# Sliding-window attention inside a two-block kernel: values as split fp32r products, probabilities scaled before the transposes

## The reference

```
scores = q . k / 8 + bias                      (bias: slope * distance, or -1e30 outside the window)
probs  = softmax([scores, sink])[..., :-1]     (the sink is in the denominator only)
out    = probs . v                             (4 query heads share one key/value head)
attn   = out * silu(gate)
y      = [pool_out, attn] @ w_out
```

## Time and profile before

| what | value |
|---|---|
| median of three runs | 1696.41 us |
| profiled execution, span from first to last instruction | 1693.7 us |
| profiled execution's own time beside its span | not on the page; the median lies 2.7 us above the span |
| TensorE busy | 1672.2 us, 99% |
| VectorE, ScalarE, GpSimd busy | 839.8, 560.5, 510.7 us |
| sliding-attention loop on TensorE | 186.5 to 321.3 us |

### The profile page before, as it was taken

The page is one execution under the profiler, slowest core; times in us unless marked ns, Lnnn a source line. Parts: engine busy times, 40 slices in busy tenths (PEclk is TensorE's granted clock), DMA queues, the critical chain, the costliest instruction groups (busy, mean ns, idle before and its releaser), DMA issues.

```text
span 1693.7 us, 22505 instructions
## 1 busy us (share of the span) xinstructions
PE 1672.2 (99%) x8729; PEld 1385.6 (82%) x8729; DVE 839.8 (50%) x1622; ACT 560.5 (33%) x1280; POOL 510.7 (30%) x402
## 2 busy tenths in 40 slices
PE   7999999999999999999999999999999999999998
PEld 6778788889888787888888887888887999988886
DVE  4330255344253624568076752838412888855714
ACT  5101456334333003440034300441113777741111
POOL 6225033023333333022220232015314745534310
PEclk9999999999999999999999999999999999999999
DMA  6113022233267232111320223126465525226322
GB/s 207 51 64 110 13 63 71 88 115 100 74 209 272 92 118 79 35 35 52 109 91 23 69 71 106 44 80 241 162 218 162 136 57 137 57 67 218 107 112 100
DMA packets 97130, 178.44 MB, mean 105 GB/s; under 512 B 13912, under 2 KB 33792, under 8 KB 96896
## 3 DMA queue, kind: packets, MB, share of 16 engines
q1 hardware_dynamic: 61120, 95.57, 19.3%
q10 hardware_dynamic: 35904, 81.44, 13.7%
HBM read 122.05 MB, written 54.92 MB: 104 GB/s over the span
## 4 chain that ended last, share of the span: by engine, by line
PE 98%; DVE 1%; ACT 1%; DMA 0%; POOL 0%; issue 0%; DVEq 0%; POOLq 0%
PE ps L1224 24%; PE ps L1138 16%; PE ps L840 14%; PE ps L1074 5%; PE ps L1387 5%; PE ps L1327 5%; PE ps L1271 4%; PE ps L976 4%; PE ps L1357 4%; PE ps L1340 3%; PE ps L894 3%; PE ps L1239 2%; PE ps L1252 2%; PE ps L1028 2%; PE ps L1001 1%; PE ps L873 1%
## 5 line engine op out<-in xcount | busy, mean ns | idle before, releaser
L720 POOL TENSOR_SCALAR w_hi<-w_stage 128x1024 fp32r<-128x1024 f32 (+3 forms) x140 | 127.8, 920 | 964.1 <-PE ps L1224 359.8
L727 POOL TENSOR_TENSOR w_lo<-w_stage,w_hi 128x1024 fp32r<-128x1024 f32 (+3 forms) x140 | 269.8, 1934 | 8.9
L1224 PE MATMUL ps<-h2T_hi,w_hi 128*128 128x512 f32 x384 | 156.6, 408 | 0.3 <-issue 0.3
L1138 PE MATMUL ps<-h2T_hi,w_hi 128*128 128x512 f32 x384 | 153.4, 399 | 0.3 <-issue 0.3
L1138 PE MATMUL ps<-h2T_lo,w_hi 128*128 128x512 f32 x384 | 152.1, 396 | 0.0
L1224 PE MATMUL ps<-h2T_hi,w_lo 128*128 128x512 f32 x384 | 152.1, 396 | 0.0
L1138 PE MATMUL ps<-h2T_hi,w_lo 128*128 128x512 f32 x384 | 151.5, 394 | 0.0
L1224 PE MATMUL ps<-h2T_lo,w_hi 128*128 128x512 f32 x384 | 151.1, 394 | 0.0
L2308 DVE SCALAR_TENSOR_TENSOR rope_swapped<-ps,sin_table_T 32x512 f32<-32x512 f32 x192 | 131.9, 687 | 3.9
L1764 ACT ACTIVATE probs_dil<-probs_dil,dil_stats_out 128x256 f32<-128x256 f32 (+2 forms) x192 | 87.5, 457 | 104.3 <-DVE dil_stats_out L2333 104.3
L2441 DVE TENSOR_REDUCE small<-ps 128x1 f32<-128x1024 f32 x64 | 77.7, 1214 | 54.9 <-PE ps L1327 54.9
(11 more groups left out here) (296 smaller groups left out, 3745.7 us busy)
## 6 DMA issues: line engine op xcount, KB each, us to landing
w_stage<-in_w_in SPq DMA_DIRECT2D x76, 512.0 KB, 3.8
w_stage<-in_w_out SPq DMA_DIRECT2D x16, 512.0 KB, 3.8
gate_scr<-gate_tiles ACTq DMA_DIRECT2D x16, 512.0 KB, 3.6
gates<-gate_scr ACTq DMA_DIRECT2D x32, 256.0 KB, 3.2
v_dil<-v_dil_scr SPq DMA_DIRECT2D x25, 256.0 KB, 3.4
v_dil_scr<-values_out SPq DMA_DIRECT2D x24, 256.0 KB, 2.0
dil_scr<-dil_out SPq DMA_DIRECT2D x96, 64.0 KB, 1.6
dil_nums<-dil_scr ACTq DMA_DIRECT2D x24, 256.0 KB, 4.2
```

The costliest lines, as they stand in the source:

```text
L720: last = nc.gpsimd.tensor_scalar(hi_, raw_, 1.0, 0.0, ALU.mult, ALU.add)
L727: last = nc.gpsimd.tensor_tensor(lo_, raw_, hi_.bitcast(F32), ALU.subtract)
L1138: m = pe.matmul(ps[:, gate_bank(u), :], a[:, s, k, P * m_:P * m_ + P], b[:, k, COLS * n:COLS * n + COLS], start=(k == 0 and j == 0), stop= ...
L1224: m = pe.matmul(bank, a, b, start=(k == 0 and i == 0), stop=(k == KT - 1 and i == 2))
```

## The change

In the sliding attention:

- V is held as a pair of fp32r tiles (`vS`), high from ScalarE, low from VectorE, side by side in one stationary tile of 128 columns per key/value head.
- VectorE forms and inverts the sums right after the exponentials (`inverse`), and GpSimd multiplies the rows of the probabilities by them (`swa_norm`), before TensorE transposes them. The four transposes of one key block go to one bank.
- ScalarE copies the transposed probabilities as fp32r (`swa_high`), and VectorE the remainder (`swa_low`), per key block.
- Values: V is stationary, and two heads' probabilities (256 columns) stream, high then low; the result has channels in partitions. It lies in two alternating banks (4 and 5), and its high and low sums in different partitions: ScalarE copies one part across partitions into `qT`, whose columns of that tile are no longer needed (`swa_merge`), VectorE adds the other (`swa_total`), GpSimd multiplies by the gate (`swa_gate`).
- No transposes back; no division after the values.
- GpSimd's new steps are placed in its queue: steps 0 to 6 ahead of panel `o0`, the rest behind single chunks of `o0` and `o1` (`SWA_STEPS`).
- The pooled half's buffer becomes single, and its pieces come at other iterations. The first tile's output products wait for two chunks of their weight panel a part, rather than for four.

```diff
-    POOL_AT = (2, 4, 6, 8, 12, 13, 14, 15)
+    POOL_AT = (2, 4, 6, 8, 12, 14, 16, 18)
+    SWA_STEPS = ((7,), (8,), (9,), (10, 11), (12,), (), (13,), (14, 15, 16, 17))
+    def swa_blocks(i):
+        return min(i, HH) + 2 * max(i - HH, 0)
...
+        def swa_norm(i):
+            t, hh = divmod(i, HH)
+            nk = P if t == 0 else 2 * P
+            pool.wait_ge(*after("swa_recip", i + 1))
+            for j in range(G):
+                h = G * hh + j
+                last = nc.gpsimd.tensor_scalar(pr[:, i % 2, j, 0:nk], pr[:, i % 2, j, 0:nk], st[:, t % 2, 1, h:h + 1], 0.0,
+                                               ALU.mult, ALU.add)
+            last.then_inc(sem("swa_normed"), 1)
+        def swa_gate(i):
+            t, hh = divmod(i, HH)
+            tk = slice(P * t, P * t + P)
+            pool.wait_ge(*after("swa_sum", i + 1))
+            pool.wait_ge(*after("fill_evac", 4 if t < 4 else 12))
+            nc.gpsimd.tensor_tensor(aT[:, hh::2, tk], aT[:, hh::2, tk], qT[:, hh::2, tk], ALU.mult).then_inc(sem("swa_aT"), 1)
+        def swa_step(i):
+            if i < TT * HH:
+                swa_norm(i)
+            if i >= 2:
+                swa_gate(i - 2)
...
+            if p == index["o0"]:
+                for i in range(7):
+                    swa_step(i)
...
+                    if p in (index["o0"], index["o1"]):
+                        for i in SWA_STEPS[4 * (p - index["o0"]) + ci]:
+                            swa_step(i)
...
         def swa_transposes(i):
-            pe.wait_ge(*after("swa_exp", G * (i + 1)))
-            if i >= 1:
-                pe.wait_ge(*after("swa_pT", i))
-            for j in range(G):
-                for kb in range(nb):
-                    c = 2 * j + kb
-                    m = pe.transpose(ps[:, 2 + c // 4, (c % 4) * P:(c % 4) * P + P],
-                                     pr[:, i % 2, j, P * kb:P * kb + P], ident[:])
-            m.then_inc(sem("swa_T"), 1)
+            pe.wait_ge(*after("swa_normed", i + 1))
+            for kb in range(nb):
+                if i >= 1:
+                    pe.wait_ge(*after("swa_lo", swa_blocks(i) - (nb - 1 - kb if i > HH else 0)))
+                for j in range(G):
+                    m = pe.transpose(ps[:, 2 + kb, P * j:P * j + P], pr[:, i % 2, j, P * kb:P * kb + P], ident[:])
+                m.then_inc(sem("swa_T"), 1)
         def swa_values(i):
-            pe.wait_ge(*after("swa_pT", i + 1))
-            if i >= 1:
-                pe.wait_ge(*after("swa_out", i))
-            for j in range(G):
-                h = swa_head(G * hh + j)
-                for kb in range(nb):
-                    kt = t - nb + 1 + kb
-                    m = pe.matmul(ps[:, 4, HD * j:HD * j + HD], pT[:, 2 * j + kb, :],
-                                  v1[:, kt, HD * (h // 4):HD * (h // 4) + HD], start=(kb == 0), stop=(kb == nb - 1))
+            pe.wait_ge(*after("swa_lo", swa_blocks(i + 1)))
+            if i == 0:
+                pe.wait_ge(*after("v1_lo", 2))
+            if i >= 2:
+                pe.wait_ge(*after("swa_sum", i - 1))
+            for kv in range(2):
+                ops = [(vS[:, t - nb + 1 + kb, kv].rearrange("p a d -> p (a d)"),
+                        p_[:, G * kb + 2 * kv:G * kb + 2 * kv + 2, :].rearrange("p j q -> p (j q)"))
+                       for kb in range(nb) for p_ in (pTh, pTl)]
+                for x_, (a, b) in enumerate(ops):
+                    m = pe.matmul(ps[:, 4 + i % 2, 2 * P * kv:2 * P * kv + 2 * P], a, b, start=(x_ == 0), stop=(x_ == len(ops) - 1))
             m.then_inc(sem("swa_valued"), 1)
-        def swa_back(t):
...
         def out_part(t, half, part):
+            if t == 0:
+                pe.wait_ge(*after("w_split", chunk_end[index[name]] - 2 * (1 - part)))
...
+        def swa_high(i):
+            for kb in range(swa_blocks(i + 1) - swa_blocks(i)):
+                act.wait_ge(*after("swa_T", swa_blocks(i) + kb + 1))
+                if i >= 1 and kb == 0:
+                    act.wait_ge(*after("swa_valued", i))
+                act.activation(pTh[:, G * kb:G * kb + G, :], ps[:, 2 + kb, :].rearrange("p (j c) -> p j c", c=P),
+                               ACT.Copy).then_inc(sem("swa_hi"), 1)
+        def swa_merge(i):
+            t, hh = divmod(i, HH)
+            act.wait_ge(*after("swa_valued", i + 1))
+            src = ps[:, 4 + i % 2, :].rearrange("p (a x q) -> p a x q", a=2, x=2)
+            tk = slice(P * t, P * t + P)
+            act.activation(qT[0:HD, hh::2, tk], src[HD:P, :, 0, :], ACT.Copy).then_inc(sem("swa_merge"), 1)
+            act.activation(qT[HD:P, hh::2, tk], src[0:HD, :, 1, :], ACT.Copy).then_inc(sem("swa_merge"), 1)
...
+        def inverse(i):
+            t, hh = divmod(i, HH)
+            hs = slice(G * hh, G * hh + G)
+            dve.wait_ge(*after("swa_sink", i + 1))
+            in_turn(nc.vector.tensor_tensor(st[:, t % 2, 1, hs], st[:, t % 2, 1, hs], st[:, t % 2, 2, hs], ALU.add))
+            nc.vector.reciprocal(st[:, t % 2, 1, hs], st[:, t % 2, 1, hs]).then_inc(sem("swa_recip"), 1)
+        def swa_low(i):
+            for kb in range(swa_blocks(i + 1) - swa_blocks(i)):
+                dve.wait_ge(*after("swa_hi", swa_blocks(i) + kb + 1))
+                js = slice(G * kb, G * kb + G)
+                nc.vector.tensor_tensor(pTl[:, js, :], ps[:, 2 + kb, :].rearrange("p (j c) -> p j c", c=P),
+                                        pTh[:, js, :].bitcast(F32), ALU.subtract).then_inc(sem("swa_lo"), 1)
+        def swa_total(i):
+            t, hh = divmod(i, HH)
+            tk = slice(P * t, P * t + P)
+            src = ps[:, 4 + i % 2, :].rearrange("p (a x q) -> p a x q", a=2, x=2)
+            dve.wait_ge(*after("swa_merge", 2 * i + 2))
+            for x_, rows in enumerate((slice(0, HD), slice(HD, P))):
+                dst = qT[rows, hh::2, tk]
+                last = nc.vector.tensor_tensor(dst, src[rows, :, x_, :], dst, ALU.add)
+            last.then_inc(sem("swa_sum"), 1)
...
-            if u >= 2:
-                act.wait_ge(*after("pool_lo", u - 1))
+            if u >= 1:
+                act.wait_ge(*after("pool_lo", u))
...
+            if 2 <= i < steps + 2:
+                swa_merge(i - 2)
             if 1 <= i <= steps:
-                swa_pT(i - 1)
+                swa_high(i - 1)
...
-        for i in range(steps + 3):
-            if i < steps:
-                softmax_in(i)
-            if 2 <= i < steps + 2:
-                normalise(i - 2)
+        for i in range(steps + 4):
+            if 1 <= i <= steps:
+                inverse(i - 1)
+            if i < steps:
+                softmax_in(i)
+            if 2 <= i < steps + 2:
+                swa_total(i - 2)
             if i - 1 in POOL_AT:
                 pool_lo(POOL_AT.index(i - 1))
             if i >= 6 and i % 2 == 0:
                 attn_lo((i - 6) // 2)
-            if i >= 4 and i % 2 == 0:
-                back((i - 4) // 2)
+            if 1 <= i <= steps:
+                swa_low(i - 1)
```

More of the change, by code:

```diff
@@ L270, in hybrid_blocks_kernel @@
     kT = sb("k1T", [P, S], F32, s2)
-    vT = sb("v1T", [P, S], F32, s2)
-    v1 = sb("v1", [P, TT, P], F32, s2)
+    vS = sb("v1_pair", [P, TT, 2, 2, HD], F32R, s2)
     swa_b = sb("swa_bias", [P, H1, 2 * P], F32, s2)
     pr = sb("probs", [P, 2, G, 2 * P], F32, s2)
-    pT = sb("probsT", [P, 2 * G, P], F32, s2)
-    ao = sb("attn_tok", [P, H1, HD], F32, s2)
+    pTh = sb("probsT_hi", [P, 2 * G, P], F32R, s2)
+    s2v = ExitStack()
+    vT = sb("v1T", [P, S], F32, s2v)
+    s2v.close()
+    pTl = sb("probsT_lo", [P, 2 * G, P], F32R, s2)
     st = sb("attn_stats", [P, 2, 4, H1], F32, s2)
-    pmR = sb("pool_outT_back", [P, 2, COLS], F32, s2)
+    pmR = sb("pool_outT_back", [P, COLS], F32, s2)
     s2.close()
@@ L984, in _ @@
         pe.wait_ge(*after("qkv_evac", 8))
-        pe.wait_ge(*after("v1_evac", 2))
         def keys_of(t):
@@ L1063, in out_part @@
                 elif t == 2:
-                    pe.wait_ge(*after("swa_pT", steps))
+                    pe.wait_ge(*after("swa_lo", swa_blocks(steps)))
                 elif t == 3:
-                    pe.wait_ge(*after("swa_out", steps))
-                    pe.wait_ge(*after("swa_aT", TT))
+                    pe.wait_ge(*after("swa_sum", steps))
                 elif half == 0:
@@ L1484, in _ @@
                 for half in range(2):
-                    act.activation(v1[:, 4 * half:4 * half + 4, :], ps[:, 4 + half, :], ACT.Copy).then_inc(sem("v1_evac"), 1)
+                    act.activation(vS[:, 4 * half:4 * half + 4, :, 0, :], ps[:, 4 + half, :].rearrange("p (t a d) -> p t a d", t=4, a=2),
+                                   ACT.Copy).then_inc(sem("v1_hi"), 1)
         def fill_evac(f):
@@ L1517, in pool_in @@
-            act.dma_start(pmR[:, u % 2, :], pool_d[P * k:P * k + P, COLS * n:COLS * n + COLS]).then_inc(sem(f"pool_back{u % 2}"), 16)
+            if u >= 1:
+                act.wait_ge(*after("pool_lo", u))
```

(27 more changed lines are left out.)

43 lines of the change are left out of this document (10 added, 33 removed).

## The result

The changed kernel took 1703.6 us (median of 5 runs, 1701.75 to 1705.6) against 1696.7 of the kernel before: ratio 1.0041, 95% interval 1.0029 to 1.0052. It is slower by 6.9 us, or 0.4%. Its profiled execution has a span of 1702.3 us, 8.6 more than before.

A forecast was written before the change was run, and what follows sets the result against it. TensorE, 98% of the chain, was taken to bound the kernel. Loop terms -0.4 + 3.4 - 4.0 + 5.6 - 2.0 = +2.6 us on 1696.4 gave 1699.0; range 1692 to 1706.

The forecast's parts named there:

- What TensorE saves: Sliding attention: cheaper values save 11.8 us, dropped transposes back 3.5, together 15.3 if nothing waits.
- Steps 8 to 11: Loop steps with two half projections: TensorE's own 8.7 us each covers the ring, so -4.0 us.
- Steps 0 to 2: Start of the sliding attention loop: cheaper first-tile values gain 0.4 us ahead of score step 3.
- Steps 16 to 18: End of the loop: two values and transposes back less, up to 0.7 us lost to last scalings, -2.0.
- Steps 3 to 7: Early loop steps: step 3 at 5.9 us, then four turns of 7.7 with hold-up; +3.4 us.
- the ring: Sliding attention loop: masking, exponentials, merges, totals, low halves, sum and reciprocal wait in a circle; 7.6 us, or 7.0.
- The second hold: Loop transposes wait for GpSimd's four scalings, 2.1 us after the low halves; step about 7.2 us even with a shorter ring.
- VectorE and GpSimd: In the loop these engines hold each other up: 0 to 0.7 us a turn, taken as 0.2; 1.8 late.
- Steps 12 to 15: Late loop steps: GpSimd's queue of scalings, gates and o1 chunks sets the length, 33.2 us against 27.6; +5.6.
- rival 2: Slower by GpSimd: scalings cost 0.56 us or merges 0.6; about +7, 1703.4 us; chance 0.34.
- Rival 1: Faster: engines hand over sooner, the ring closes in 6.6 us and chunks fit between; -8.6, 1687.8 us; chance 0.17.
- Rival 3: TensorE's clock falls in the loop's new gaps, its work taking 11.8 us a step; +33, 1729 us; chance 0.03.

The follow-up runs named there:

- e6: e8 with VectorE's low halves moved ahead of the masking and ScalarE's high copies ahead of the merges; 1684.2 us.
- e1: Changed kernel with VectorE reordered (masking, low halves of step i-2, totals of step i-3) and GpSimd's gate products one step later; 1692.5 us.
- e0: Changed kernel with VectorE's pooled or attention low half moved behind the low halves of the probabilities; 1700.9 us.
- e4: Changed kernel without GpSimd's scalings, so rows are not divided by their sums; 1701.4 us.
- e7: Changed kernel with the reorderings of e1 and e2 together and without GpSimd's scalings; 1690.1 us.
- e2: Changed kernel with only GpSimd's order changed: gate products one step later, panel o1's four chunks ahead of scalings 11 to 14; 1700.1 us.
- e8: Changed kernel with the reorderings of e1 and e2 together, plus VectorE's pooled or attention low half ahead of the totals; 1686.6 us.

## Why the prediction was right and wrong

The mechanism was as forecast in steps 3 to 7 and only in part in the late steps, and its size was short: 1699.0 against 1703.6, inside the range. "Within 0.2%" was the likeliest of the three outcomes, and the kernel came out 0.4% slower. By its steps:

- **What TensorE saves**: right. Eight values take 0.96 (322.47 in the chain) for the forecast 0.94. With most of its waits gone (e6), 12.7 of the 15.3 us come out as time.
- **Steps 8 to 11**: -4.0 forecast, -4.0 measured. **Steps 0 to 2**: -0.4 and -0.4. **Steps 16 to 18**: -2.0 and -1.6.
- **Steps 3 to 7**: +3.4 forecast, +5.2 measured: step 3 took 6.5 instead of 5.9, the four turns 32.0 instead of 30.8. This is the step that failed most by size: the ring was the right cause (e1, e0), but 7.6 should have been 8.19, and 7.0 without the low half 7.47. Masking with its add took 2.03 (forecast 1.90), the merges 0.79 (0.65), the totals 0.86 (0.70), the low half beside them 0.7 (0.6). I took a tenth off each pair for overlap; in this chain no pair overlapped (two merges of 0.38 and 0.39 took 0.79), and each handover added some 0.02 to 0.1. The exponentials' rows make 2.18, not the 2.15 of my sum; they took 2.17. The eight steps that can move had a mean of 8.23 instead of 8.0.
- **The second hold**: wrong as a bound. Its terms make 2.0 and 6.9, not 2.1 and 7.2, and the turn that it was to set is the ring's 7.47. Scalings at 0.46 instead of 0.40 make it no shorter, but e4 shows that without them the turn loses 0.1, and e7 that the open step loses nothing. The 9.2 us put down to them in the waits are the ring's.
- **VectorE and GpSimd**: 0.2 a turn forecast in steps 4 to 7, 0.1 measured (the add at 214.62, 0.28 instead of 0.16); in the late steps 1.8 in all forecast, 3.1 measured, and there it moves with the order of either engine (e2, e8).
- **Steps 12 to 15**: +5.6 forecast, +6.3 to 6.4 measured, for another reason, so that the near miss is in part luck. I took GpSimd for the only bound there, "busy without a pause". In the trace it pauses twice for 2.2 us, for VectorE's reciprocal, and TensorE waits for o1's split for only 0.8 in all: what paces these steps is the ring, with two hold-ups in it (e2), and GpSimd's queue is the next bound (e1). Within GpSimd's sum, what failed is "counted from scores 12": I let the chunk start 5.2 us in, behind scaling 11, and overlooked that the gate product of step 8 waits for the last Silu ahead of it; it started after 6.8. e2 prices that and the order at 3.2. The 0.5 that the sum holds for two bare weight loads has no row.
- **Rivals**: rival 2 gave the right time, 1703.4, for the wrong reason: scalings cost 0.46 and not 0.56, merges 0.38 and not 0.6. Rival 1's mechanism (the ring closing sooner) did not come. Rival 3's clock did fall, to 0.96 over steps 3 to 7 and 0.90 over steps 12 to 15; a clock under 1.00 was one of my signs of being wrong. Two stretches of the changed kernel:
```profile
228.00:232.00 4.00, 2.62 (x16) 2.23 (x16) 2.48 (x12) 1.92 (x7) 2.55 (x5) 0.87 0.20 70
232.00:236.00 4.00, 4.00 (x17) 2.71 (x17) 2.34 (x5) 3.11 (x10) 0.00 (x0) 0.70 0.00 0
```
After 1.4 us of idle time in 4, the granted clock is 0.70 over the next 4, in which TensorE is busy throughout: part of them at 1.2 GHz, the lower level. The ring did not notice: turns are 8.19 from 220.34 (clock 1.00) and 8.19 from 228.53 (0.79). In the late steps eight transposes and the scores behind them fall into such a stretch:
```profile
299.32 1.97 PE L1058 MATMUL ps<-ident,probs 128*128 128x128 f32 x8 [2.12 <-POOL probs L790]
301.22 1.84 PE L1046 MATMUL ps<-k1T,q1T 64*128 64x256 f32 x8
303.47 0.51 PE L1108 MATMUL ps<-w_hi,mixT_hi 128*128 128x512 f32 x1 [0.41 <-POOL w_lo L741]
```
At full clock they take 1.09 and 1.13 in the same kernel. But behind them TensorE waits 0.41 for o1's split, and the turn of the ring around them, from 297.25, is 8.26, no longer than the 8.28 to 8.31 of steps 8 to 11 at full clock: these 1.6 us are not on the path. My row for the rival, the first 20 us of the earlier trace rows, was no safe witness against it. The Trainium skill (TensorE: Matmul & The Clock Gate, "Why this matters for your kernels") speaks of longer idle gaps between bursts than the waits here, so I was wrong to call the rival likelier by it. The clock fell all the same, and it cost far less than the 33 us of that rival.
- **A misread row**: the earlier trace rows has GpSimd busy for 0.0 to 14.3 us of a stretch, not for 3.7 and more; nothing in the sum rests on it.

## What to carry to other kernels

Before an edit shortens the engine that bounds a loop, follow one value of each other engine from turn to turn: if the way through their in-order queues closes on itself, its length is the new step wherever it is longer than that engine's own, and the sum must be made of full durations with a start for each handover. What held up an instruction on this ring was added to its turn in full (the 1.0 and 2.0 us of e2). Reordering can break the ring with no instruction left out: here the reordered queues of VectorE, GpSimd and ScalarE turned +6.9 us into -12.7 (e6). A wait that a profile puts down to the last instruction of a chain does not say that this instruction sets its length: taking it away (e4) moved the time by 2.2 us, where 9.2 were put down to it.

## What was not expected of the hardware

A 128x4 sum on VectorE took 1.43 us instead of 0.16, and a 128x512 subtraction 2.71 to 2.86 instead of 0.69, beside a subtraction of GpSimd. The cost followed the order of issue and not the amount of work: with GpSimd's order changed (e2) it was gone from two such instructions, and with less work on GpSimd (e7) the loop was 2.6 us longer, in part perhaps by TensorE's lower clock.
